# Causal masks added to the decay rows by GpSimd, and both halves of the sample's probabilities in one matmul operand

## What is computed

```
z = rmsnorm(x, g_mix) @ w_in            # columns: pool u | q | k | v | forget logits
c = cumsum(log_sigmoid(z_f + b_f))      # over cached and new tokens
s = q k^T / 8 + (c[query] - c[key])     # per head
s = where(query_pos >= key_pos, s, -inf)
o = softmax(s) @ v
```

## Time and profile before

| | |
|---|---|
| median of 3 runs | 936.68 us (936.23 to 942.18) |
| the profiled execution | 937.53 us, of it the span of instructions 935.7 us |
| PE busy | 893.0 us (95%) |
| DVE busy | 522.0 us (56%) |
| ACT busy | 357.9 us (38%) |
| POOL busy | 54.9 us (6%) |
| mean granted TensorE clock | 0.994 |

### The profile page before, as it was taken

The page is one execution under the profiler, slowest core; times in us unless marked ns, Lnnn a source line. Parts: engine busy times, 40 slices in busy tenths (PEclk is TensorE's granted clock), DMA queues, the critical chain, the costliest instruction groups (busy, mean ns, idle before and its releaser), DMA issues.

```text
span 935.7 us, 16494 instructions
## 1 busy us (share of the span) xinstructions
PE 893.0 (95%) x6386; PEld 855.9 (91%) x6386; DVE 522.0 (56%) x941; ACT 357.9 (38%) x574; POOL 54.9 (6%) x96
## 2 busy tenths in 40 slices
PE   4989999999899899999999999999999999999996
PEld 3888999999799679998999999999999999999996
DVE  4365676675576446556667655632555642355644
ACT  5255455444743445344234333311233321133324
POOL 4012101022100002000000000000000000000000
PEclk9999999999999999999999999999999999999999
DMA  6236323212632554320122323233322233222122
GB/s 198 67 89 169 98 86 92 70 46 95 186 90 87 212 203 123 97 69 23 47 88 91 90 69 88 67 91 89 89 68 87 70 90 90 85 73 81 59 84 103
DMA packets 116860, 88.89 MB, mean 95 GB/s; under 512 B 3168, under 2 KB 107830, under 8 KB 116819
## 3 DMA queue, kind: packets, MB, share of 16 engines
q1 hardware_dynamic: 111683, 71.15, 25.9%
q0 software_dynamic: 5136, 17.17, 6.0%
HBM read 81.32 MB, written 6.99 MB: 94 GB/s over the span
## 4 chain that ended last, share of the span: by engine, by line
PE 84%; DVE 5%; DMA 4%; ACT 4%; issue 2%; SPq 0%; DVEq 0%; ACTq 0%
PE ps L378 66%; PE ps L1704 3%; PE ps L1566 2%; PE ps L1632 2%; DMA w_raw<-in_w_mk 2%; PE ps L1863 2%; ACT w_hi L389 1%; DVE w_lo L394 1%; PE ps L1892 1%; PE ps L1675 1%; DMA w_raw<-in_w_mv 1%; PE ps L1913 1%; PE ps L1633 1%; DMA x_tok<-in_x_prompt 1%; DVE y_tok L1530 1%
## 5 line engine op out<-in xcount | busy, mean ns | idle before, releaser
L394 DVE TENSOR_TENSOR w_lo<-w_raw,w_hi 128x1024 fp32r<-128x1024 f32 x124 | 152.6, 1230 | 207.5 <-ACT w_hi L389 205.4
L378 PE MATMUL ps<-a_hi,w_hi 128*128 128x288 f32 x1024 | 222.9, 299 | 3.1 <-DVE w_lo L394 1.8
L378 PE MATMUL ps<-a_lo,w_hi 128*128 128x288 f32 x1024 | 220.1, 297 | 0.0
L378 PE MATMUL ps<-a_hi,w_lo 128*128 128x288 f32 x1024 | 220.0, 297 | 0.0
L389 ACT ACTIVATE w_hi<-w_raw 128x1024 fp32r<-128x1024 f32 x124 | 130.8, 1055 | 226.1 <-PE ps L378 180.6
L378 PEld LDWEIGHTS ps<-a_hi,w_hi 128*128 128x128 f32 x1024 | 165.9, 190 | 5.4 <-DVE w_lo L394 1.2
L378 PEld LDWEIGHTS ps<-a_hi,w_lo 128*128 128x128 f32 x1024 | 165.9, 190 | 0.0
L378 PEld LDWEIGHTS ps<-a_lo,w_hi 128*128 128x128 f32 x1024 | 165.8, 190 | 0.0
L378 PE MATMUL ps<-b_hi,w_hi 128*128 128x288 f32 x576 | 124.1, 297 | 0.8 <-DVE b_lo L401 0.8
L378 PE MATMUL ps<-b_lo,w_hi 128*128 128x288 f32 x576 | 123.3, 296 | 0.0
L378 PE MATMUL ps<-b_hi,w_lo 128*128 128x288 f32 x576 | 123.3, 296 | 0.0
(11 more groups left out here) (358 smaller groups left out, 1272.6 us busy)
## 6 DMA issues: line engine op xcount, KB each, us to landing
w_raw<-in_w_up SPq DMA_DIRECT2D x44, 512.0 KB, 3.8
w_raw<-in_w_in SPq DMA_DIRECT2D x16, 512.0 KB, 4.1
w_raw<-in_w_down SPq DMA_DIRECT2D x16, 512.0 KB, 3.7
w_raw<-in_w_o SPq DMA_DIRECT2D x8, 512.0 KB, 3.8
w_raw<-in_w_mk SPq DMA_DIRECT2D x8, 512.0 KB, 3.3
w_raw<-in_w_mv SPq DMA_DIRECT2D x8, 512.0 KB, 3.3
w_raw<-in_w_mq SPq DMA_DIRECT2D x8, 512.0 KB, 3.7
w_raw<-in_w_mo SPq DMA_DIRECT2D x8, 512.0 KB, 3.7
```

The source lines that it names most:

```text
L378: mm = nc.tensor.matmul(acc[:, h, 0:H], w[slot][:, c], x[:, k, h * H:h * H + H], start=(k == first and w is w_hi and x is x_hi), stop=(k = ...
L394: nc.vector.tensor_tensor(w_lo[slot][:], w_raw[slot][:], w_hi[slot][:].bitcast(F32), ALU.subtract).then_inc(weight_lo_ready, 1)
```

## The change

The mask matmuls are gone. GpSimd adds the causal tile to the decay rows in SBUF. As a query tile's diagonal block is masked and the same block serves unmasked for later tiles, the row is loaded once for each query tile, cut to its keys: blocks of 1, 2, 3 and 4 tiles, 10 in all for each head, by four DMAs. Two heads fit (`decay_p` is [128, 2, 10, 128] in place of [128, 2, 2, 512]): the buffer of a head is free again when its four entries of the pair before are taken. DVE waits for `decay_ready` at entries 0 and 4, and for `decay_s_ready` at entry 8.

The transposed probabilities lie as [128, buffer, key tile, hi or lo, 128], so that for the sample the values' hi half is multiplied by both halves in one matmul of 256 columns (as before, the values' lo half by the hi half alone, 128 columns). The two results lie in two column ranges of the bank, so DVE adds them into `o_sum`, and ACT and DVE split `o_sum` in place of the bank.

```diff
-            def load_decay_prompt(j):
-                if j >= 2:
-                    pool.wait_ge(scores_taken, ENTRIES * (j - 2) + 2 * NT)
-                for h in range(2):
-                    row = decay_p_dram[2 * j + h:2 * j + h + 1, :]
-                    pool.dma_start(decay_p[:, j % 2, h, :], row.partition_broadcast(P)).then_inc(decay_landed[j % 2], 16)
+            def load_decay(j, h):
+                if j >= 1:
+                    pool.wait_ge(scores_taken, ENTRIES * (j - 1) + NT * (h + 1))
+                for t in range(NT):
+                    row = decay_p_dram[2 * j + h:2 * j + h + 1, 0:t * P + P]
+                    pool.dma_start(decay_p[:, h, DIAGONAL[t]:DIAGONAL[t + 1], :].rearrange("p c q -> p (c q)"),
+                                   row.partition_broadcast(P)).then_inc(decay_landed[h], 16)
+
+            def mask_decay(j, h):
+                pool.wait_ge(decay_landed[h], 16 * NT * (j + 1))
+                for t in range(NT):
+                    block = decay_p[:, h, DIAGONAL[t] + t, :]
+                    ins = nc.gpsimd.tensor_tensor(block, block, causal[:], ALU.add)
+                ins.then_inc(decay_ready[h], 1)
+
+            def mask_sample(j):
+                pool.wait_ge(decay_s_landed, 32 * (j + 1))
+                pool.wait_ge(masks_split, 2)
+                nc.gpsimd.tensor_tensor(decay_s[:, PAST:KEYS], decay_s[:, PAST:KEYS], causal_s[:],
+                                        ALU.add).then_inc(decay_s_ready, 1)
...
-            load_decay_prompt(0)
+            load_decay(0, 0)
+            load_decay(0, 1)
             load_cache(0)
+            mask_decay(0, 0)
             load_sample(0)
-            load_decay_prompt(1)
+            mask_decay(0, 1)
+            mask_sample(0)
             for j in range(1, PAIRS):
+                load_decay(j, 0)
                 load_cache(j)
+                load_decay(j, 1)
+                mask_decay(j, 0)
+                mask_decay(j, 1)
                 load_sample(j)
-                if j + 1 < PAIRS:
-                    load_decay_prompt(j + 1)
+                mask_sample(j)
...
                 if out is not None:
                     n, g = out
-                    act.wait_ge(pv_done, g + 1)
+                    if n % OUTPUTS == 2:
+                        act.wait_ge(o_sum_ready, n // OUTPUTS + 1)
+                    else:
+                        act.wait_ge(pv_done, g + 1)
                     for d, b in output_pieces(n):
                         ins = copy(d(b_hi), b)
...
                 if out is not None:
+                    if out[0] % OUTPUTS == 2:
+                        dve.wait_ge(pv_done, out[1] + 1)
+                        both = OB[:, out[0] % 2]
+                        for h in range(2):
+                            r = slice(h * DH, h * DH + DH)
+                            ins = nc.vector.tensor_copy(o_sum[r, :], both[r, P + h * DH:P + h * DH + TS])
+                        after(ins)
+                        for h in range(2):
+                            r = slice(h * DH, h * DH + DH)
+                            ins = nc.vector.tensor_tensor(o_sum[r, :], o_sum[r, :], both[r, h * DH:h * DH + TS], add)
+                        ins.then_inc(o_sum_ready, 1)
                     dve.wait_ge(o_hi_ready, out[0] + 1)
                     for d, b in output_pieces(out[0]):
                         ins = minus(d(b_lo), b, f32(d(b_hi)))
...
                         for q, kk in ((q_hi, k_hi), (q_hi, k_lo), (q_lo, k_hi)):
-                            mm(bank[:, 0:w], q[r, b, c], kk[r, b, 0:w], start=(q is q_hi and kk is k_hi), stop=False)
-                        ins = mm(bank[:, c], ident_r[:], causal_r[:], start=False, stop=True)
+                            ins = mm(bank[:, 0:w], q[r, b, c], kk[r, b, 0:w], start=(q is q_hi and kk is k_hi), stop=(q is q_lo))
...
+                            rows = P if eg < ENTRIES - 1 else TS
+                            v = [x[:, at_c, :] for x in (vc_hi, vc_lo)] if eg < ENTRIES - 1 else [x[:, feats] for x in (own_hi, own_lo)]
+                            if at_c < n_all - 1:
+                                mm(out, v[0], pt[0:rows, t % 2, c], start=(at_c == 0), stop=False)
+                            ins = mm(out[:, 0:P], v[1], pt[0:rows, t % 2, c, 0], start=False, stop=False)
+                            if at_c == n_all - 1:
+                                ins = mm(out, v[0], pt[0:rows, t % 2, c], start=False, stop=True)
```

More of the change, by code:

```diff
@@ L144, in build @@
         inv_rms = place("inv_rms", [P, T])
-        logf = place("logf", [HEADS, T])
+        o_sum = place("o_sum", [P, TS])
         a_last = place("a_last", [P, 4, NF])
@@ L150, in build @@
         phase = here[0]
+        here[0] = at["b_lo"]
+        logf = place("logf", [HEADS, T])
+        here[0] = phase
         v_hi = place("v_hi", [P, NT, DFOX], F32R)
@@ L163, in build @@
         k_new = place("k_new", [P, PAIRS, T])
-        decay_p = place("decay_p", [P, 2, 2, TP])
+        DIAGONAL = [(t * (t + 1)) // 2 for t in range(NT + 1)]
+        decay_p = place("decay_p", [P, 2, DIAGONAL[NT], P])
         decay_s = place("decay_s", [P, KEYS])
         prob_p = place("prob_p", [P, 4, TP])
-        pt_hi = place("pt_hi", [P, 2, TP], F32R)
-        pt_lo = place("pt_lo", [P, 2, TP], F32R)
+        pt = place("pt", [P, 2, NT, 2, P], F32R)
         vc_hi = place("vc_hi", [P, CT, P], F32R)
@@ L190, in build @@
         hist_tok = place("hist_tok", [16, DPOOL])
-        causal = place("causal", [P, P])
         here[0] = at["b_hi"]
@@ L224, in build @@
         pool_tok = place("pool_tok", [NHIST, 2, DPOOL])
-        assert here[0] >= at["prob_p"]
+        here[0] = max(here[0], at["prob_p"])
         sum_c = place("sum_c", [P, U_S + TS])
         sum_d = place("sum_d", [P, U_S + TS])
-        assert here[0] <= at["pt_hi"]
+        assert here[0] <= at["pt"]
         here[0] = at["decay_p"]
@@ L231, in build @@
         assert here[0] <= at["pool_tok"]
-        here[0] = at["pt_hi"]
+        here[0] = at["pt"]
         wp_raw = place("wp_raw", [P, GROUPS, P])
@@ L889, in _ @@
                             act.wait_ge(pv_done, last_prob_turn(t) + 1)
-                        copy(pt_hi[0:rows, t % 2, 0:width], TB[t % 2][0:rows, 0:width]).then_inc(turn_hi_ready, 1)
+                        copy(pt[0:rows, t % 2, 0:width // P, 0, :],
+                             TB[t % 2][0:rows, 0:width].rearrange("p (c q) -> p c q", q=P)).then_inc(turn_hi_ready, 1)
                 if s < N_ENTRIES and e == ENTRIES - 1:
@@ L1640, in _ @@
                         for q, kk in ((qs_hi, k_hi), (qs_hi, k_lo), (qs_lo, k_hi)):
-                            mm(bank[:, 0:TS], q[:, b, :], kk[:, b, TP:T], start=(q is qs_hi and kk is k_hi), stop=False)
-                        ins = mm(bank[:, 0:TS], ident_r[:], causal_s[:], start=False, stop=True)
+                            ins = mm(bank[:, 0:TS], q[:, b, :], kk[:, b, TP:T], start=(q is qs_hi and kk is k_hi), stop=(q is qs_lo))
                     ins.then_inc(scores_done, 1)
@@ L1696, in _ @@
                         at_c = n_0 + c
-                        for vx, px in ((0, pt_hi), (0, pt_lo), (1, pt_hi)):
-                            if eg < 2 * NT:
-                                v, pp = (v_hi, v_lo)[vx][:, c, feats], px[:, t % 2, c * P:c * P + P]
-                            elif eg < ENTRIES - 1:
-                                v, pp = (vc_hi, vc_lo)[vx][:, at_c, :], px[:, t % 2, c * P:c * P + P]
-                            else:
-                                v, pp = (own_hi, own_lo)[vx][:, feats], px[0:TS, t % 2, 0:P]
-                            ins = mm(out, v, pp, start=(at_c == 0 and vx == 0 and px is pt_hi),
-                                     stop=(at_c == n_all - 1 and vx == 1))
+                        if eg < 2 * NT:
+                            for vx, px in ((0, 0), (0, 1), (1, 0)):
+                                ins = mm(out, (v_hi, v_lo)[vx][:, c, feats], pt[:, t % 2, c, px, :],
+                                         start=(c == 0 and vx == 0 and px == 0), stop=(c == n_all - 1 and vx == 1))
+                        else:
+                            rows = P if eg < ENTRIES - 1 else TS
[5 more added lines that the diff above has]
+                                ins = mm(out, v[0], pt[0:rows, t % 2, c], start=False, stop=True)
                     ins.then_inc(pv_done, 1)
```

28 lines of the change are left out of this document (13 added, 15 removed).

## The result

The changed kernel takes 956.56 us (median of 4 runs, 955.97 to 958.08) against 936.72 (4 runs, 936.23 to 942.18): ratio 1.021, 95% interval 1.018 to 1.024. It is slower by 19.8 us; 936.1 was forecast. The profiled execution took 956.58, its span 954.8 (before 935.7).

A forecast was written before the change was run, and what follows sets the result against it. PE was taken to bound the loop, so a removed matmul counts only while PE arrives last. Terms -0.3 + 0.24 - 0.55 + 0 = -0.6 gave 936.9 profiled, 936.1 against the median; range 931.5 to 940.

The forecast's parts named there:

- Work taken from PE: Attention loop: mask matmuls removed and 0.10 us less for each key tile of the sample's values, in all 9.1 us.
- A period of pairs 1 and 2, +0.12: Stretches of one period, cut at PE's places, summed to +0.12 us; pairs 1 and 2 together +0.24.
- the stretch with q: From entry 1's transposes to the projection for the next pair's k: waiting for `o_sum` delays PE, +1.07 us.
- Pair 3, -0.55: Last pair, copies of u in place of q: +0.4 us instead of +1.07, with the other four terms -0.55.
- behind the loop 0: Region after the attention loop: values save 0.9 us on PE, `o_sum` operations put 0.9 at its beginning; zero.
- Start of pair 0, -0.3: Pair 0: eight masks count -1.28 us, later landing of the cached keys costs 1.0; total -0.3.
- 0.77 MB more are 3.9 us: Start of pair 0: extra bytes ahead of the cached keys, at 195 GB/s, move their landing from 77.0 to 80.9.
- First scores at 77.3, hidden with 0.1 to spare: Start of pair 0: DVE takes first scores at 77.3, not 75.00, done at 77.6; PE's third scores need them at 77.7.
- Rival 4: Start: keys land 2 us late or more, first scores wait for their mask past 78; +3, 939 us; chance 0.11.
- Rival 3: PE's waits at k projections and cached keys lower the clock if above 2 us; 941.8 us; chance 0.10.

The follow-up runs named there:

- masks_only: The changed kernel with the values and the sample's output as before, masks still added by GpSimd and decay rows loaded by query tile: 949.93 us.
- pieces_before: The kernel before with only the first pair's decay rows loaded in 4 pieces of 128 columns for each head, same bytes: 940.99 us.
- values_only: The kernel before with only the change's second half (both probability halves in one operand, `o_sum` added by DVE), masks and loads as before: 936.75 us.
- values_early: values_only with DVE's four `o_sum` operations moved ahead of its `pt_lo` in their step: 933.89 us.
- filler_all: The changed kernel with 9, 31 and 17 matmuls of unused result in PE's waits at the start of the first pair: 947.85 us.

## Why the prediction was wrong

- *Work taken from PE.* Right: 72 matmuls, 0.10 a key tile. Of the 1.4 us of masks in a period 0.78 reach the end in masks_only.
- *A period of pairs 1 and 2, +0.12.* Right in each stretch but one: between the starts on either side -0.12, -0.39, -0.13, then +1.28 for +1.07, -0.08 and 0.00, sum +0.56. The `o_sum` operations took 0.93 for 0.9, but a signal from DVE to PE took 0.15 (139.96 + 0.45 to 140.56), where I had 0.05 from no row. The size that was off is the stretch with q.
- *Pair 3, -0.55; behind the loop 0.* Measured 0.0 and -0.5. Together as forecast.
- ***Start of pair 0, -0.3.*** This step failed; it was +15.5. "The queues moved 195 GB/s there ... so 0.77 MB more are 3.9 us": that rate was taken from the kernel before, with decay rows of 2 KB, and the loads by tile, eight with rows of 0.5 to 2 KB, moved 126 GB/s in their first 5 us, with the queues nearly as full. I priced bytes and issues at the old rate. Even at 126 GB/s the 0.77 MB would be an estimated 6.1 us, and the keys would land at 83.1; they landed at 87.8, 13.9 us after their issue and not 6.1, and that remainder of 4.7 us is open. "First scores at 77.3, hidden with 0.1 to spare" became 80.98. GpSimd's stand of 3.40 us was in no term, and an add took 0.42, not 0.3. The low clock behind the waits of 3.51 and 4.02 was in no term of the sum either. The Trainium skill's page "DMA: Bandwidth & Descriptors" ("Specifications") puts the limit of the full rate at 512 bytes, and by that limit alone the rows would have been harmless; pieces_before, with rows of just that length, moved 151 GB/s where whole rows moved 227, though its larger number of loads has a part in that.
- *Rival 4* had the mechanism (keys 2 us late or more, scores past 78) and +3 for it. It was sized without the clock.
- *Rival 3*, "decides between 1.4 and 2.1 us of wait": wrong in both directions. The low clock followed a wait of 1.11 us in values_only and one of 1.51 in pair 2 of the changed kernel, not the same 1.51 in its pair 1, nor 1.40 behind the loop; and the 2.12 at the start was followed by none in values_early. And its price was taken from the shortest case, 2.6 us at half clock after a wait; after 3.51 and 4.02 it was 23.9. By the Trainium skill's page "TensorE: Matmul & The Clock Gate" ("Why this matters for your kernels") the waits of 1.1 and 1.5 would have cost none; here they did.

So the 15.7 us that the first pair lost (49.51 less 33.81) are, by one profiled execution of each kernel, 11.0 for late rows and keys and 5.6 more at the low clock (7.1 less 1.5), less 0.9 for the masks; by the slower executions of filler_all the clock has less of it. How the 11.0 divide between decay rows and keys I can't say, since each trial that made one earlier left the other late. The 1.4 us in the last part of the run lie with a stretch of 3.4 us at half clock at 331; that other kernels have it too in some runs is all that was seen, its cause is open.

## What to carry to other kernels

When a load is cut into pieces and grows by it, do not price its bytes alone at the old rate: count the issues, mind the length of rows that are read for all partitions, compare GB/s with the share of the queues in a window, and look at what is queued behind it. Ahead of a stage in which PE is the bound, a late load cost twice here, once as a wait and once as the clock that follows, so the first use of a mask is the wrong place to save 0.16 us; keep the old way there and take the gain where loads are long landed. And a gain on PE that lies just ahead of a wait for DVE is no gain: put new DVE work into an idle gap that the timeline shows, before counting it.

## What was not expected of the hardware

- Packets of 4096 bytes on GpSimd's queue took 264 ns with two loads in rows of 2 KB and 518 to 673 ns with eight loads in rows of 512 bytes to 2 KB (pieces_before and after); the keys' packets, in pieces of 512 bytes as well, took 227.
- GpSimd stood for 3.40 us ahead of the tenth load of the stage (4.46 in pieces_before), and with a larger ring not at all.
- The granted clock answers to PE's idle time and not to useful work: idle matmuls in a gap of 2 us removed the low stretch behind it. How long that stretch lasts varied between profiled executions of nearly equal starts, from none (values_early) over 3.4 us (before) to 13.7 (values_only), and with it the first pair from 32.9 to 38.3 us. Over the runs of the kernel before the time went with the mean granted clock: on one chip the fastest, 933.60, had 0.997 and the slowest, 942.14, 0.984.
